# Weights of v for two chunks at a time, one-hot rows for eight tokens in two steps, and h in blocks of 32 tokens

## The reference

```
q = einsum('td,de->te', xc, wq)...             # 8 heads, 2 halves of 128
s = einsum('thpd,hpnd->thpn', q, sub_keys)     # scores against 128 keys of each half
sv, si = top_k(s, 16)                          # 16 best keys of each half
cand = sv[..., 0, :, None] + sv[..., 1, None, :]
top, pos = top_k(cand, 16)                     # 16 best pairs of keys: experts of 16384
g = softmax(top)
a = gelu(einsum('thkd,td->thk', u[eidx], xc))
out = einsum('thk,thkd->td', g * a, v[eidx])
```

## Time and profile before

| | |
|---|---|
| median of 3 runs | 1568.46 us (1567.51 to 1569.08) |
| span of the profiled execution | 1565.4 us |
| PE busy | 1527.4 us, 98% |
| PE weight loads busy | 1363.9 us, 87% |
| DVE busy | 1337.7 us, 85% |
| ACT busy | 660.1 us, 42% |
| POOL busy | 487.5 us, 31% |

### The profile page before, as it was taken

The page is one execution under the profiler, slowest core; times in us unless marked ns, Lnnn a source line. Parts: engine busy times, 40 slices in busy tenths (PEclk is TensorE's granted clock), DMA queues, the critical chain, the costliest instruction groups (busy, mean ns, idle before and its releaser), DMA issues.

```text
span 1565.4 us, 24588 instructions
## 1 busy us (share of the span) xinstructions
PE 1527.4 (98%) x8275; PEld 1363.9 (87%) x8275; DVE 1337.7 (85%) x2877; ACT 660.1 (42%) x1143; POOL 487.5 (31%) x450
## 2 busy tenths in 40 slices
PE   4999999999999999999999999999999999999997
PEld 4887767888999999999999999999999998888886
DVE  5788666549999989899698898899999998999977
ACT  3444554233344757657433333343333332333232
POOL 1121300033450000020355455456566663233000
PEclk9999999999999999999999999999999999999999
DMA  9754410132355565676899999999999999999772
GB/s 366 270 174 148 148 68 0 55 95 82 118 169 180 194 230 199 229 248 251 298 393 330 350 340 343 346 337 371 372 378 372 368 345 355 376 350 352 241 244 104
DMA packets 160467, 398.77 MB, mean 255 GB/s; under 512 B 11753, under 2 KB 75369, under 8 KB 158705
## 3 DMA queue, kind: packets, MB, share of 16 engines
q1 hardware_dynamic: 112992, 227.06, 41.7%
q0 software_dynamic: 36864, 134.23, 23.2%
q10 hardware_dynamic: 10514, 36.30, 5.9%
HBM read 359.27 MB, written 38.27 MB: 254 GB/s over the span
## 4 chain that ended last, share of the span: by engine, by line
PE 83%; DVE 13%; DMA 1%; ACT 1%; issue 1%; ACTq 0%; DVEq 0%; SPq 0%
PE bank_S L907 16%; PE bank_T L907 11%; PE bank_O L858 6%; PE bank_O L856 6%; PE bank_O L857 6%; PE bank_T L885 5%; PE bank_G L907 5%; PE bank_S L856 3%; PE bank_S L857 3%; PE bank_S L858 3%; PE bank_O L643 2%; PE bank_S L610 2%; DVE mod_acc L1909 1%; DVE v_sb L1902 1%; DVE v_sb L1915 1%; DVE si L1921 1%
## 5 line engine op out<-in xcount | busy, mean ns | idle before, releaser
L1462 ACT ACTIVATE v_hi<-v_raw 128x1024 fp32r<-128x1024 f32 x124 | 131.7, 1062 | 333.9 <-PE bank_G L907 330.9
L1434 ACT ACTIVATE u_hi<-u_raw 128x1024 fp32r<-128x1024 f32 x128 | 135.9, 1061 | 243.0 <-PE bank_O L858 122.8
L1213 POOL COPY stage<-eidx 128x1 uint32<-128x1 uint32 (+1 forms) x128 | 75.7, 591 | 461.8 <-DVE eidx L2030 207.7
L1217 POOL DMA_INDIRECT row<-in_peer_u,stage x128 | 148.1, 1157 | 103.8 <-POOL stage L1213 103.8
L856 PE MATMUL bank_S<-h_hi,u_hi 128*128 128x384 f32 x512 | 179.7, 351 | 0.5 <-DVE u_lo L2002 0.5
L858 PE MATMUL bank_O<-h_hi,u_lo 128*128 128x384 f32 x512 | 171.9, 336 | 0.0
L856 PE MATMUL bank_O<-h_hi,u_hi 128*128 128x384 f32 x512 | 171.7, 335 | 0.0
L858 PE MATMUL bank_S<-h_hi,u_lo 128*128 128x384 f32 x512 | 171.5, 335 | 0.0
L857 PE MATMUL bank_O<-h_lo,u_hi 128*128 128x384 f32 x512 | 171.5, 335 | 0.0
L857 PE MATMUL bank_S<-h_lo,u_hi 128*128 128x384 f32 x512 | 171.4, 335 | 0.0
L2098 DVE SCALAR_TENSOR_TENSOR y<-row,wgt,y 128x1024 f32<-128x1024 f32 x128 | 165.9, 1296 | 0.0
(11 more groups left out here) (370 smaller groups left out, 3647.8 us busy)
## 6 DMA issues: line engine op xcount, KB each, us to landing
u_raw<-in_u_t SPq DMA_DIRECT2D x128, 512.0 KB
v_raw<-in_peer_v SPq DMA_DIRECT2D x128, 512.0 KB
gates<-g_out ACTq DMA_DIRECT2D x12, 2048.0 KB, 6.8
g_in<-gates SPq DMA_DIRECT2D x32, 768.0 KB
ada_late<-in_w_ada SPq DMA_DIRECT2D x8, 2048.0 KB, 8.4
spill<-a_act ACTq DMA_DIRECT2D x56, 192.0 KB, 2.1
a_act<-spill SPq DMA_DIRECT2D x14, 768.0 KB, 10.6
w_raw<-in_w_in SPq DMA_DIRECT2D x20, 512.0 KB, 4.1
```

The lines of the kernel that those rows point to most:

```text
L1217: pool.indirect_dma_start(rows[slot][:, :], None, table[:, :], bass.IndirectOffsetOnAxis(stage[:, place:place + 1], 0))\
L1434: act.activation(u_hi[c % 2][:, :], u_raw[:, c % 2, :], ACT.Copy).then_inc(s_uhi, 1)
L1462: act.activation(v_hi_end[:, i % TAIL, :] if end else v_hi[:, c % 2, :], v_raw[c % 4][:, :], ACT.Copy)\
```

## The change

Four things change.

1. The one-hot rows. One tile `hot` of 2 x 8 x 128 elements, with two buffers, holds hot_i and hot_j of eight tokens. DVE compares all 2048 elements in one instruction, waits for it, and multiplies the first 1024 with the gates in place. PE's group of four tokens waits for the eight it belongs to.
2. The weights of v. `product` multiplies the gelus of two chunks (768 elements) with the gates, in place in `g_in`, on DVE one chunk ahead (at the odd chunks). ACT copies them to the high part (`w_high`, after the gelu of each even chunk), DVE subtracts the low part (`w_low`, at the start of the even chunk). The high and low parts get two buffers of two chunks. A load of g_in now waits until the low parts of what stands in it are made.
3. The dots of tile 0 write into the row of u that they read instead of into `junk`.
4. h_hi and h_lo are laid out as 16 blocks x 8 x 32 tokens, so a matmul over 384 tokens reads 12 runs of 32 elements.

Several tiles get other places. u_lo of odd chunks moves into h_lo's place of tile 0, and POOL's first split into it waits for the last query.

```diff
-        h_hi = at("h_hi", 32, [P, NT, KD, P], f32r)
+        h_hi = at("h_hi", 32, [P, S // GB, KD, GB], f32r)
...
-        g_in = at("g_in", 56, [P, 2, DT // GB, 4, GB])
+        g_in = [at(f"g_in{j}", kib, [P, DT // GB, 4, GB]) for j, kib in enumerate((56, 182))]
...
-        hot_j = at("hot_j", 128, [P, 2, 4, P])
-        hot_i = at("hot_i", 132, [P, 2, 4, P])
-        w_f = at("w_f", 128, [P, DT])
-        w_hi = at("w_hi", 130, [P, 2, DT], f32r)
-        w_lo = at("w_lo", 133, [P, 2, DT], f32r)
+        hot = [at(f"hot{j}", kib, [P, 2, 8, P]) for j, kib in enumerate((128, 176))]
+        w_hi = [at(f"w_hi{j}", kib, [P, 2, DT], f32r) for j, kib in enumerate((128, 194))]
+        w_lo = [at(f"w_lo{j}", kib, [P, 2, DT], f32r) for j, kib in enumerate((176, 179))]
...
-                    pe.matmul(ps[:, 0:DT], u_hi[q][:, kk], h_hi[:, GT:NT, k, :], start=(k == 0), stop=False)
+                    pe.matmul(ps[:, 0:DT], u_hi[q][:, kk], h_hi[:, GT * P // GB:S // GB, k, :], start=(k == 0), stop=False)
...
-                        pe.wait_ge(s_hot, B + 1)
+                        pe.wait_ge(s_hot, B // 2 + 1)
                         for tok in range(4):
-                            mm = pe.matmul(ps[:, tok * P:tok * P + P], hot_j[:, b % 2, tok, :], hot_i[:, b % 2, tok, :],
-                                           start=True, stop=True)
+                            own = hot[B // 2 % 2][:, :, 4 * (B % 2) + tok, :]
+                            mm = pe.matmul(ps[:, tok * P:tok * P + P], own[:, 1, :], own[:, 0, :], start=True, stop=True)
...
-                    after(sp, s_pw, 4 * (q - 1))
+                    after(sp, s_w, 2 * (q - 1))
...
+            def w_high(i, c):
+
+                if not within(i):
+                    return
+                if at_end(i):
+                    act.wait_ge(s_acc, PH * TOPK)
+                else:
+                    after(act, s_yv, i - 2)
+                act.wait_ge(s_pw, over(i, c, 2) + 1)
+                act.activation(weight_pair(w_hi, w_hi_end, i, c), gate_pair(c), ACT.Copy).then_inc(s_whi, 1)
...
+                if c % 2 == 0:
+                    w_high(m + 2, c + 2)
...
-                for B in range(tile * P // 4, (tile + 1) * P // 4):
-                    after(dve, s_gm, B - 1)
-                    for tok in range(4):
-                        n = 4 * B + tok
-                        dve.tensor_scalar(hot_i[:, B % 2, tok, :], iota_k[:, :], cols[:, 0, n:n + 1],
-                                          cols[:, 2, n:n + 1], ALU.is_equal, ALU.mult)
-                    dve.tensor_tensor(hot_j[:, B % 2, :, :], iota_k[:, :].unsqueeze(1).to_broadcast([P, 4, P]),
-                                      cols[:, 1, 4 * B:4 * B + 4].unsqueeze(2).to_broadcast([P, 4, P]),
-                                      ALU.is_equal).then_inc(s_hot, 1)
-                    if B % 4 == 3:
-                        split_u(BETWEEN[tile].stop + B // 4 - 8 * tile + 1)
+                for B in range(tile * P // 8, (tile + 1) * P // 8):
+                    after(dve, s_gm, 2 * (B - 1))
+                    tokens, both = slice(8 * B, 8 * B + 8), hot[B % 2]
+                    done(dve, dve.tensor_tensor(both[:, :, :, :],
+                                                iota_k[:, :].unsqueeze(1).unsqueeze(1).to_broadcast([P, 2, 8, P]),
+                                                cols[:, 0:2, tokens].unsqueeze(3).to_broadcast([P, 2, 8, P]),
+                                                ALU.is_equal), s_dv)
+                    dve.tensor_tensor(both[:, 0, :, :], both[:, 0, :, :],
+                                      cols[:, 2, tokens].unsqueeze(2).to_broadcast([P, 8, P]), ALU.mult)\
+                       .then_inc(s_hot, 1)
+                    if B % 2:
+                        split_u(BETWEEN[tile].stop + B // 2 - 8 * tile + 1)
...
+            def product(i, c):
+
+                if not within(i):
+                    return
+                late = isinstance(i, int) and i >= MAIN
+                dve.wait_ge(s_g[c // 4 % 2], 16 * (over(i, c, 8) + 1))
...
+                slot = c % AHEAD
+                dve.tensor_tensor(gate_pair(c), by_block(a_act[:, slot:slot + 2, :]), gate_pair(c), ALU.mult)\
+                   .then_inc(s_pw, 1)
+
+            def w_low(i, c):
+
+                dve.wait_ge(s_whi, over(i, c, 2) + 1)
+                if not at_end(i):
+                    after(dve, s_yv, i - 2)
+                dve.tensor_tensor(weight_pair(w_lo, w_lo_end, i, c), gate_pair(c),
+                                  weight_pair(w_hi, w_hi_end, i, c).bitcast(f32), ALU.subtract).then_inc(s_w, 1)
...
-                weigh(i, c, late)
+                if c % 2 == 0:
+                    w_low(i, c)
+                else:
+                    product(i + 1, c + 1)
```

More of the change, by code:

```diff
@@ L184, in peer_block_kernel @@
         u_hi = [at(f"u_hi{j}", kib, [P, D], f32r) for j, kib in enumerate((88, 80))]
-        u_lo = [at(f"u_lo{j}", kib, [P, D], f32r) for j, kib in enumerate((92, 84))]
+        u_lo = [at(f"u_lo{j}", kib, [P, D], f32r) for j, kib in enumerate((92, 64))]
         v_hi = at("v_hi", 112, [P, 2, D], f32r)
@@ L308, in after, with half_columns, gate_pair, by_block @@
             eng.wait_ge(s, n)
+        def half_columns(h, i, half):
+            return h[:, i * P // GB:i * P // GB + P // GB, 4 * half:4 * half + 4, :].rearrange("p n a t -> p a n t")
+        def gate_pair(c):
+            return g_in[c // 4 % 2][:, :, c % 4:c % 4 + 2, :].rearrange("p b i t -> p i b t")
+        def by_block(pair):
+            return pair.rearrange("p i (b t) -> p i b t", t=GB)
+        def weight_pair(w, w_end, i, c):
+            if at_end(i):
+                q = i % TAIL
+                return by_block(w_end[:, q:q + 2, :])
+            return by_block(w[c // 2 % 2][:, :, :])
         def within(i, last=NCHUNK - 1):
@@ L804, in q_passes @@
             def q_passes(e, tiles):
+                blocks = slice(tiles.start * P // GB, tiles.stop * P // GB)
                 ps = bank[f"S{e % 3}"][:, tiles.start * P:tiles.stop * P]
@@ L810, in q_passes @@
                     kk = slice(k * P, k * P + P)
-                    pe.matmul(ps, wq_hi_of(e)[:, kk], h_hi[:, tiles, k, :], start=(k == 0), stop=False)
-                    pe.matmul(ps, wq_hi_of(e)[:, kk], h_lo[:, tiles, k, :], start=False, stop=False)
-                    mm = pe.matmul(ps, wq_lo[e % 2][:, kk], h_hi[:, tiles, k, :], start=False, stop=(k == KD - 1))
+                    pe.matmul(ps, wq_hi_of(e)[:, kk], h_hi[:, blocks, k, :], start=(k == 0), stop=False)
+                    pe.matmul(ps, wq_hi_of(e)[:, kk], h_lo[:, blocks, k, :], start=False, stop=False)
+                    mm = pe.matmul(ps, wq_lo[e % 2][:, kk], h_hi[:, blocks, k, :], start=False, stop=(k == KD - 1))
                 return mm
@@ L897, in v_chunk @@
             def v_chunk(i, c):
-                pe.wait_ge(s_w, i + 1)
+                pe.wait_ge(s_w, over(i, c, 2) + 1)
                 pe.wait_ge(s_vlo, i + 1)
-                q = c % 2
+                q, pair = c % 2, c // 2 % 2
                 first = isinstance(i, int) and i == 0
@@ L906, in v_chunk @@
                         for half in range(2):
-                            mm = pe.matmul(y_bank[t][half][:, :], w[:, q, tt], v[:, q, half * 512:half * 512 + 512],
+                            mm = pe.matmul(y_bank[t][half][:, :], w[pair][:, q, tt],
+                                           v[:, q, half * 512:half * 512 + 512],
                                            start=(first and n == 0), stop=False)
@@ L920, in chunk_ready @@
                 def chunk_ready(m):
-                    pe.wait_ge(s_w, m + 1)
+                    pe.wait_ge(s_w, m // 2 + 1)
                     pe.wait_ge(s_vlo, m + 1)
@@ L1198, in split_u @@
                     return
+                if i == 1:
+                    taken(pool, ("q", 2 * PH - 1))
                 pool.wait_ge(s_uhi, i + 1)
@@ L1523, in _ @@
             act.wait_ge(s_gst[1], 16 * (BLOCKS // 2))
+            w_high(0, 0)
             def parts(m, c, late, numbers):
@@ L1543, in squares @@
                 to = ss[:, 2 * NT + i:2 * NT + i + 1] if half is None else half_ss[:, 2 * i + half:2 * i + half + 1]
-                act.activation(rows[0][:, part], x_sb[:, i, part], ACT.Square, accum_out=to).then_inc(s_f2, 1)
+                act.activation(rows[2][:, part], x_sb[:, i, part], ACT.Square, accum_out=to).then_inc(s_f2, 1)
             def std(i):
@@ L2120, in chunk @@
                     dve.wait_ge(s_got[2 * place], 16 * (over(n, g, RING) + 1))
-                    dve.scalar_tensor_tensor(out=junk[:, :], in0=rows[2 * place][:, :], scalar=1.0, in1=h2[:, 0, :],
+                    dve.scalar_tensor_tensor(out=rows[2 * place][:, :], in0=rows[2 * place][:, :], scalar=1.0,
+                                             in1=h2[:, 0, :],
                                              op0=ALU.mult, op1=ALU.mult, accum_out=dots[:, g % 4:g % 4 + 1])\
```

(1 more changed line is left out.)

45 lines of the change are left out of this document (14 added, 31 removed).

## The result

The changed kernel takes 1591.74 us (median of 4 runs, 1589.57 to 1592.98) beside 1568.77 us of the kernel before on the same chip: ratio 1.0147, 95% interval 1.0132 to 1.0161, or 23 us more. The span of the profiled execution is 1587.8 us, 22.4 more than the 1565.4 of before. The forecast was 1580: the sign is right, the size (11.5 us) is half of what came.

The account below looks back on a forecast made before the run. PE was taken to bound the v loop, PE and DVE level in the gate stretches. 11.0 us there and 0.5 at the turn, others 0, made 11.5: span 1565.4 to 1576.9, median 1580; range from 1574 to 1593.

Parts of the forecast that it names:

- What bounds each stage: In the v loop PE sets the pace and DVE has room; in the three gate stretches PE and DVE run level.
- The gate stretches, 11.0 us: Making one-hot rows for eight tokens, DVE becomes slower than PE; delays of 3.48, 3.77 and 3.77 us in three tiles.
- keeps level: Gate stretches: the pair costs 3.31 us or less, only each tile's first group is late; 1574 us, chance 0.15.
- The turn, 0.54 us: Between the gates' landing and the first v matmul, product, copy and low part make PE wait 0.54 us.
- The v loop, 0: Weights made for two chunks at a time, partly on ACT, cost PE nothing in the v loop; 0 us.
- Its cover: v loop: 1.6 us free for ACT's extra 0.85, product a chunk ahead; without it up to 24 us.
- The rival on w_high: w_high holds up ACT in the fast part of the v loop; up to 1604 us, chance 0.03.
- h in blocks of 32: Matmuls over h reading runs of 32 were taken to cost 0, bounded by 13.4 us slower and 46 us faster.
- my upper bound of 13.4: Matmuls over h: one column (0.42 ns) for each of 32,100 further runs, 13.4 us at most.
- the bounded rival, Runs cost a column each: Matmuls over h: each further run costs one column, 0.42 ns; 1593 us, chance 0.07.
- full speed in every slice: The prediction's reading of PE's granted clock before the change, over the whole span: the 2.4 GHz level.

## Why the prediction was half right

**What bounds each stage** held. DVE's 71 us less in the v loop brought nothing, and in the gate stretches, where DVE has no spare time, its longer steps cost.

**The gate stretches, 11.0 us**, held: 11.6 us by the medians with this part alone. From DVE's first compare to the last group of a tile I had 65.9 us; the changed kernel shows 66.06, 66.08 and 66.86 (511.08 to 577.14 in the first), the one-hots alone 66.75, 66.73 and 65.99. The tiles near 66.0 are the forecast's; the others have 0.7 us on top, from the clock (last section). In the changed kernel this part and the blocks of 32 overlap: with the blocks alone PE takes 7.84 us for sixteen tokens instead of 7.75, still less than DVE's 8.06, so the slower matmuls over h cost nothing within these tiles. DVE's rival, "keeps level", asked for a pair of 3.31 us or less; it takes 3.47. The estimate of 3.32 us for the pair, from the price in the Trainium skill (VectorE: DVE Perf Modes, "The TRN2 errata"), is 0.15 us too low in this trace. Nearly all of that is the product's start, 2.33 us behind the compare where the price gives 2.19.

**The turn, 0.54 us**: its steps held, its wait depends on when the gates land. 1.19 us without the other parts, none in the changed kernel.

**The v loop, 0** held for PE in the changed kernel. Its cover is thinner than I wrote: I named the gates' load as needed a chunk sooner and missed that the reloaded gelus are too. That is the one wait of 1.0 us with this part alone. The rival on w_high did not come: no wait of PE in these traces goes back to it.

**h in blocks of 32: "I take 0, the nearest row."** This is the step that failed, and the matmuls' 173 ns moved to 177.4, which the prediction itself named as a sign of being wrong. The term is worth 11.3 us by the ratio and 11.9 by the medians, against my upper bound of 13.4: in the profiled execution 3.3 us in the queries (first query to first chunk of u, 104.04 us before, 303.60 to 410.97 with blocks of 32, 107.37) and 9.5 over the chunks of u. The ground for 0 was that 384 columns in 3 runs and 512 in one carry the same 13 ns. That says that runs of 128 are free, and nothing of short ones; no row had a run under 128, and the bounded rival got 0.07. "Runs cost a column each" gave 1593 and so came within 2 us of the time, but partly by luck, since its law is not right either: blocks of 64 would have cost 4.5 us by it and cost nothing, 9 more runs of 32 in 384 columns cost 4.4 ns where it has 3.8, and 12 more in 512 cost 9 where it has 5. That there is a price and what it is was measured; by what path TensorE reads its operand was not.

With 11.3 in place of 0 the forecast would have been 1591.

The versions that undo the loss reach the kernel before and no more: with h in 64 or 128 and four-token one-hots it is 1568 to 1570 us. None beat it, which fits a kernel in which PE is busy 98% of the span.

## What to carry to other kernels

A new access pattern of a matmul's moving operand is a change to PE's own time, the one engine that has no cover here; when no row of the trace has runs as short, a bounded price must weigh as much as 0, and a kernel with the layout alone is the first thing to run. Runs of 64 fp32r elements were free here (0.9998, and 1.0002 with near jumps), runs of 32 cost 0.7 to 0.9%: lay out such an operand so that a run holds 64 or more. For a producer that runs level with its consumer, add up its steps over a whole period with the wait between dependent steps in it: what it loses there sets the end, and a sooner start gives nothing back.

## What was not expected of the hardware

The price of short runs, above: 384 columns in fp32r take 173 ns in 1, 3 or 6 runs, 177 to 180 in 12, 181 in 24, and 512 columns take 227 ns in 4 runs and 236 in 16.

The clock. After the 2.2 us wait before the third tile PE ran for 3.4 us at a granted clock of 0.50, the 1.2 GHz level, and its matmuls of 384 columns stood 0.32 us apart (by stretch, columns as before, and two rows of PE's timeline):

```profile
697.00:700.00 3.00, 0.83 (x5) 0.52 (x4) 2.97 (x3) 1.43 (x2) 2.89 (x2) 1.00 0.85 322
700.00:701.00 1.00, 0.99 (x9) 1.00 (x9) 1.00 (x1) 0.00 (x0) 0.28 (x1) 0.96 0.97 102
701.00:703.00 2.00, 2.00 (x9) 2.00 (x8) 1.97 (x2) 1.08 (x1) 1.90 (x1) 0.50 0.83 305
...
704.00:706.00 2.00, 2.00 (x15) 2.00 (x14) 1.76 (x2) 1.12 (x1) 1.18 (x3) 0.92 0.83 295
```

```profile
701.34 0.52 PE L873 MATMUL bank_S<-h_lo,u_hi 128*128 128x384 f32 x1
701.66 0.52 PE L874 MATMUL bank_S<-h_hi,u_lo 128*128 128x384 f32 x1
```

The same wait had no such effect in the first two tiles. With the one-hots alone it did in the first and second tile, and in the changed kernel with h in 128 in the second and third: 5 of 9 waits of 2.2 us in these three traces, and none in the kernel whose waits are 1.2 us at most. Each cost a tile 0.7 us, less than PE lost: DVE went on meanwhile and waited for PE only 0.6 us (`DVE hot L2089` in the waits above). What decides it was not tried. The page does not show such a stretch: each slice of `PEclk` is 39 us long, and its 9 means 90% or more. So "full speed in every slice", as the prediction reads it, is too much even before the change, where the clock stood at 0.63 in the mean from 30 to 44 us.
